# A mixture-of-experts encoder step: one 128-slot expert in the middle, experts in a table's order, 8 KB rows for the down weights

## What is computed

```
logits = h @ w_router + b_router                      # [384, 32]
top_val, top_idx = lax.top_k(logits, 4)               # 4 of 32 experts for each token
gates = softmax(top_val)
# for each expert e that a token chose:
gu = xblk @ w_gate_up[e] + b_gate_up[e]               # [1024] -> [2048]
x_glu, x_lin = jnp.split(gu, 2, axis=-1)              # clamped at 7
act = x_glu * sigmoid(1.702 * x_glu) * (x_lin + 1.0)
y += gates * (act @ w_down[e] + b_down[e])            # [1024] -> [1024]
```

## Time and profile before

| | us |
|---|---|
| median of 3 runs | 1396.67 |
| the profiled execution | 1392.92 |
| its span, first to last instruction | 1391.1 |
| PE busy | 1257.7 (90%) |
| DVE busy | 410.3 (29%) |
| ACT busy | 233.4 (17%) |
| weight loads, queue 1 | 77.6% of 16 DMA engines' span |

### The profile page before, as it was taken

How to read it: one execution, slowest core, us unless ns; L and a number is a source line. 1 busy time by engine, 2 the same in 40 slices (tenths; PEclk the granted TensorE clock), 3 DMA queues, 4 the chain that set the end, 5 groups by cost and what they waited for, 6 DMA issues and landing times.

```text
span 1391.1 us, 16030 instructions
## 1 busy us (share of the span) xinstructions
PE 1257.7 (90%) x5950; PEld 601.2 (43%) x5950; DVE 410.3 (29%) x849; ACT 233.4 (17%) x455; POOL 176.4 (13%) x153
## 2 busy tenths in 40 slices
PE   3997689899899999999999999999999999999696
PEld 2564468775734434334343324434333443425232
DVE  3496853411441321213212122221212222121223
ACT  0117634323211011010110101001010101100002
POOL 1099824325300000000000000000000000000000
PEclk8998699889799999999999999999999999999898
DMA  9222022003699999999999999999999999999991
GB/s 322 82 81 90 11 82 76 1 8 140 231 399 418 418 418 418 418 416 417 418 418 418 418 417 417 418 418 418 419 417 416 417 418 418 418 418 416 417 391 54
DMA packets 91374, 446.13 MB, mean 321 GB/s; under 512 B 9072, under 2 KB 14448, under 8 KB 57456
## 3 DMA queue, kind: packets, MB, share of 16 engines
q1 hardware_dynamic: 87168, 436.66, 77.6%
q10 hardware_dynamic: 3376, 5.99, 1.3%
q0 software_dynamic: 800, 3.08, 0.7%
HBM read 441.05 MB, written 4.65 MB: 320 GB/s over the span
## 4 chain that ended last, share of the span: by engine, by line
PE 45%; DMA 23%; SPq 18%; DVE 4%; issue 4%; POOL 3%; ACT 2%; ACTq 0%; DVEq 0%; POOLq 0%
DMA ring<-in_w_gate_up 22%; PE bank L1542 11%; SPq L413 10%; PE bank L1562 8%; SPq L417 8%; PE bank L1510 7%; PE bank L1228 5%; PE bank L1435 3%; DMA win<-in_w_in 2%; POOL ring L351 2%; PE bank L1524 2%; POOL cb L475 1%; DVE qkvc L858 1%; PE bank L1315 1%; PE bank L1336 1%
## 5 line engine op out<-in xcount | busy, mean ns | idle before, releaser
L1542 PE MATMUL bank<-ring,win 128*64 128x512 f32 x2112 | 480.6, 598 | 42.6 <-DMA ring<-in_w_gate_up 42.5
L1542 PEld LDWEIGHTS bank<-ring,win 128*64 128x64 f32 x2112 | 143.5, 137 | 361.2 <-issue 222.4
L1562 PE MATMUL bank<-ring,win 128*64 128x512 f32 x1056 | 239.5, 607 | 1.6 <-issue 0.8
L1116 DVE TENSOR_SCALAR win<-bank 128x512 f32<-128x512 f32 x33 | 22.8, 692 | 706.7 <-PE bank L1542 706.7
L1228 PE MATMUL bank<-hT,win 128*128 128x384 f32 x384 | 132.9, 508 | 20.7 <-DMA win<-in_w_in 9.6
L1562 PEld LDWEIGHTS bank<-ring,win 128*64 128x64 f32 x1056 | 74.7, 139 | 152.5 <-issue 149.7
L1228 PEld LDWEIGHTS bank<-hT,win 128*128 128x128 f32 x384 | 76.1, 200 | 75.2 <-issue 17.0
L770 ACT ACTIVATE win<-win 128x512 f32<-128x512 f32 x32 | 20.2, 630 | 500.8 <-DVE win L1116 500.8
L1510 PEld LDWEIGHTS bank<-win,qkvc 128*128 128x128 f32 x816 | 95.9, 196 | 14.3 <-issue 13.0
L1510 PE MATMUL bank<-win,qkvc 128*128 128x128 f32 (+1 forms) x816 | 100.4, 281 | 1.2 <-DVE win L1051 1.2
L1524 PE MATMUL bank<-win 128*128 128x512 f32 x192 | 89.2, 601 | 0.8 <-DVE win L1194 0.8
(11 more groups left out here) (269 smaller groups left out, 923.4 us busy)
## 6 DMA issues: line engine op xcount, KB each, us to landing
ring<-in_w_gate_up SPq DMA_DIRECT2D x264, 1024.0 KB, 20.5
ring<-in_w_down SPq DMA_DIRECT2D x132, 1024.0 KB, 22.9
win<-in_w_in SPq DMA_DIRECT2D x4, 2048.0 KB, 8.2
win<-in_w_in SPq DMA_DIRECT2D x4, 1024.0 KB, 17.9
win<-in_w_out SPq DMA_DIRECT2D x2, 2048.0 KB, 9.4
out_ss<-ring POOLq DMA_DIRECT2D x1, 2048.0 KB, 11.9
hT<-in_xT SPq DMA_DIRECT2D x1, 1536.0 KB, 10.7
out_y<-xt SPq DMA_DIRECT2D x3, 512.0 KB, 2.7
```

The source lines that it names most:

```text
L1542: mm = pe.matmul(bank[half][a * BLK:(a + 1) * BLK], xs[:, k], ring[:, c:c + 512], start=False, stop=(k == KD - 1), skip_group_check=True)
L1562: mm = pe.matmul(bank[7][a * BLK:(a + 1) * BLK], actT[:, (k % 4) * P + (k // 4) * BLK:][:, 0:BLK], ring[:, c:c + 512], start=(k == 0), sto ...
```

## The change

The pairs become 15 (`NPAIR`), in 17 units (`NU`): units 0 to 7 are pairs at positions 0 to 15, unit 8 (`MID`) is one expert with 128 slots at position 16 (`WIDE`), units 9 to 15 are pairs at positions 17 to 30, and unit 16 is one expert of 64 slots at position 31. DVE finds the fullest of experts 2 to 31 (`places_of_units`) and swaps it with expert 16; a table `expert_no` gives the expert of each position, and SP reads an entry of it before each turn's loads from position 2 on. The fullest expert no longer counts as over 64 in the table of extra blocks (over 128 it still would). The extra loops stand behind unit 14 as before, now counted with `s_tabs` 2. In the wide unit each k multiplies both halves of the slots before its ring slot is released, into banks 0, 1, 4 and 5; its `down` writes banks 7 and 3. A down slot's partition p gets rows 2p and 2p+1, one piece of 8 KB, and `turn_act` reads the columns of `a_s` two apart to match.

```
-NPAIR = NE // 2
+NPAIR = (NE - 2) // 2
+NU = NPAIR + 2
+MID = NPAIR // 2 + 1
+WIDE = 2 * MID
...
+        a_rows = a_s.rearrange("p (b r two) -> p b r two", b=2, two=2)
...
+        WIDE_COMBINE = (2, 3, 0, 1, 2, 3)
+        WIDE_BANK = 3
```

SP, the loads:

```
-                        src = w_down[bass.ds(e, 1), r0:r0 + 2 * P, :].rearrange("a (k p) n -> (a p) k n", p=P)
-                        ld.dma_start(dst.rearrange("p (k n) -> p k n", k=2), src).then_inc(s_w[s], 16)
+                        src = w_down[bass.ds(e, 1), r0:r0 + 2 * P, :].rearrange("a (p k) n -> (a p) (k n)", p=P)
+                        ld.dma_start(dst, src).then_inc(s_w[s], 16)
...
-            with sp.Fori(1, NE - 2) as e:
-                load_expert(sp, e, lambda s: e * USES + (USED[s] - USES))
-
+            load_expert(sp, 1, lambda s: USED[s])
             sp.wait_ge(s_tabs, 1)
+            with sp.Fori(2, NE - 3) as e:
+                number = sp.value_load(expert_no[0:1, bass.ds(e, 1)], min_val=0, max_val=NE - 1)
+                load_expert(sp, number, lambda s: e * USES + (USED[s] - USES))
+
...
+            for e in (NE - 3, NE - 2, NE - 1):
+                number = sp.value_load(expert_no[0:1, e:e + 1], min_val=0, max_val=NE - 1)
+                load_expert(sp, number, lambda s: n_extra * USES + ((e - 1) * USES + USED[s]))
```

DVE and (the first six lines) ACT:

```
+            def wide_unit():
+                sigmoid(2 * MID)
+                sigmoid(2 * MID + 1)
+                rows_high(MID + 1)
+                gates_t(MID)
+                rows_out(0, 7, WIDE)
+                rows_out(1, WIDE_BANK, WIDE)
...
+            def places_of_units():
+                link(dve.memset(big[:, 0:2], 0.0))
+                link(dve.scalar_tensor_tensor(key, cntB, 2.0 * NE, iota[:, 0:NE], ALU.mult, ALU.subtract))
+                link(dve.tensor_reduce(topkey, key[:, 2:NE], AX_X, ALU.max))
+                link(dve.tensor_scalar(big[:, 2:NE], key[:, 2:NE], topkey, None, ALU.is_equal))
+                link(dve.tensor_scalar(rest, big, -1.0, 1.0, ALU.mult, ALU.add))
...
+                link(dve.tensor_scalar(expert_at[:, WIDE:WIDE + 1], bigno, float(WIDE), None, ALU.add))
+                link(dve.tensor_copy(expert_no, expert_at))
+                dve.tensor_scalar(sel_at[0:3 * NE], expert_at[0:3 * NE], cst[0:3 * NE, X_ROW:X_ROW + 1], None,
+                                  ALU.is_equal).then_inc(s_tabs, 1)
...
+                link(dve.tensor_tensor(nxb, nxb, rest, ALU.mult))
...
+            def wide_unit():
+                dve.wait_ge(s_hp, MID + 1)
+                gate_hits_one(WIDE, P)
+                dve.wait_ge(s_hg, MID + 1)
+                dve.wait_ge(s_xg5, MID + 1)
+                row_hits(pos_at, WIDE + 1)
+                clamp(WIDE, s_g, s_lin)
+                swiglu(s_sig, item + 1, s_g, item + 1, s_lin, item * 2 + 2, s_act)
+                turned(s_att, item + 1, s_atr)
+                clamp(WIDE, s_g, s_lin, low=4)
+                for o in (0, 1):
+                    add(o, WIDE_COMBINE[o], s_cmb, MID * 6 + (o + 1), s_add)
+                swiglu(s_sig, item + 2, s_g, item + 2, s_lin, item * 2 + 4, s_act)
+                for o in range(2, 6):
+                    add(o, WIDE_COMBINE[o], s_cmb, MID * 6 + (o + 1), s_add)
+                turned(s_att, item + 2, s_atr, to=actT_wide)
...
+            places_of_units()
+            pair(0, 0, 0, lambda: row_hits(pos_at, 2), (2, 3), tables)
+            with dve.Fori(1, MID - 1) as u:
+                pair(u, 2 * u, 2 * u, lambda: row_hits(pos_at, 2 * u + 2), (2 * u + 2, 2 * u + 3))
+            pair(MID - 1, WIDE - 2, WIDE - 2, lambda: row_hits_one(WIDE, P), (WIDE, WIDE))
+            wide_unit()
+            with dve.Fori(MID + 1, NU - 2) as u:
+                pair(u, 2 * u - 1, 2 * u - 1, lambda: row_hits(pos_at, 2 * u + 1), (2 * u + 1, 2 * u + 2))
```

PE:

```
-                    mm = pe.transpose(bank[6][:, j * P:(j + 1) * P], a_s[:, j * P:(j + 1) * P], mat("ident"))
+                    mm = pe.transpose(bank[6][:, j * P:(j + 1) * P], a_rows[:, j // 2, :, j % 2], mat("ident"))
...
+            def wide_unit():
+                for x in range(2):
+                    bias_rows(sel_sb[:, x], bank[4 * x], 0)
+                    bias_rows(sel_sb[:, x], bank[4 * x + 1], F)
+                for k in range(KD):
+                    pe.wait_ge(s_w[SLOT_OF[k]], WIDE * 16 + 16)
+                    for x in range(2):
+                        for half in range(2):
+                            for a in range(2):
+                                c = SLOT_OF[k] * SLOT + half * F + a * 512
+                                mm = pe.matmul(bank[4 * x + half][a * BLK:(a + 1) * BLK], xTe[:, k, x * BLK:(x + 1) * BLK],
+                                               ring[:, c:c + 512], start=False, stop=(k == KD - 1), skip_group_check=True)
+                                if k == KD - 1 and x == 1:
+                                    mm.then_inc(s_wu, 1)
+                    if k < KD - 1:
+                        mm.then_inc(s_wu, 1)
+                pe.wait_ge(s_gtc, MID)
+                pe.wait_ge(s_yc, item * 2)
+                pe.wait_ge(s_add, MID * 6)
+                for o in (0, 1):
+                    combine(o, gT, y_s, s_cmb, WIDE_COMBINE)
+                turn_act(s_act, item + 1, s_att)
+                for o in (2, 3):
+                    combine(o, gT, y_s, s_cmb, WIDE_COMBINE)
+                pe.wait_ge(s_add, MID * 6 + 2)
+                for o in (4, 5):
+                    combine(o, gT, y_s, s_cmb, WIDE_COMBINE)
+                pe.wait_ge(s_hp, MID + 2)
+                pe.wait_ge(s_lin, item * 2 + 3)
+                rows(range(6), hp, P)
+                pe.wait_ge(s_atr, item + 1)
+                turn_act(s_act, item + 2, s_att)
+                rows(range(6, KD), hp, P).then_inc(s_xg5, 1)
+                pe.wait_ge(s_atr, item + 2)
+                pe.wait_ge(s_hg, MID + 1)
+                turn_gates()
+                pe.wait_ge(s_add, MID * 6 + 6)
+                for k in range(KD):
+                    if k % 2 == 0:
+                        pe.wait_ge(s_w[KD + k // 2], WIDE * 16 + 16)
+                    for x, (aT, b) in enumerate(((actT, 7), (actT_wide, WIDE_BANK))):
+                        for a in range(2):
+                            c = (KD + k // 2) * SLOT + (k % 2) * D + a * 512
+                            mm = pe.matmul(bank[b][a * BLK:(a + 1) * BLK], aT[:, (k % 4) * P + (k // 4) * BLK:][:, 0:BLK],
+                                           ring[:, c:c + 512], start=(k == 0), stop=(k == KD - 1), skip_group_check=True)
+                            if k == KD - 1 and x == 1:
+                                mm.then_inc(s_wu, 1)
+                    if k % 2 == 1 and k < KD - 1:
+                        mm.then_inc(s_wu, 1)
...
+            pair(0, True, 0)
+            with pe.Fori(1, MID) as u:
+                pair(u, False, 2 * u)
+            wide_unit()
+            with pe.Fori(MID + 1, NU - 2) as u:
+                pair(u, False, 2 * u - 1)
...
+            pair(NU - 2, False, n_extra + (NE - 3), ahead=BLK)
+            item, turn = 2 * NU - 2, n_extra + (NE - 1)
+            first_expert(NU - 1, False, turn)
+            pe.wait_ge(s_atr, item + 1)
+            pe.wait_ge(s_hg, NU)
+            turn_gates()
+            down(turn, s_atr, item + 1)
+            pe.wait_ge(s_gtc, NU)
+            pe.wait_ge(s_yc, item * 2 + 2)
+            pe.wait_ge(s_add, 6 * NU)
             for o in range(6):
-                combine(o, gT, y_s, s_cmb)
+                combine(o, gT[0:BLK], y_s[0:BLK], s_cmb)
```

More of the change, by code:

```diff
@@ L197, in stream_step @@
         xTe = wscratch(KD * P).rearrange("p (k s) -> p k s", k=KD)
-        g_s, l_s, sg_b, t_s, a_s, actT = (wscratch(512) for _ in range(6))
+        g_s, l_s, sg_b, t_s, a_s, actT, actT_wide = (wscratch(512) for _ in range(7))
+        a_rows = a_s.rearrange("p (b r two) -> p b r two", b=2, two=2)
         y_s = wscratch(D).rearrange("p (a n) -> p a n", a=2)
@@ L221, in stream_step @@
         if8 = srow(NT * 8).rearrange("p (n j) -> p n j", n=NT)
-        gate = srow(NT * NE).rearrange("p (n e) -> p n e", n=NT)
+        both = srow(2 * NT * NE).rearrange("p (q e) -> p q e", q=2 * NT)
+        pos, gate = both[:, 0:NT], both[:, NT:2 * NT]
+        placed = srow(2 * NT * NE).rearrange("p (q e) -> p q e", q=2 * NT)
+        pos_at, gate_at = placed[:, 0:NT], placed[:, NT:2 * NT]
+        big, rest, key = srow(NE), srow(NE), srow(NE)
+        topkey, bigno = srow(1), srow(1)
+        expert_at = srow(NE)
+        expert_no = srow(NE).bitcast(I32)
+        sel_at = srow(NE)
+        swap = cb[:, NX * NE:NX * NE + 2 * NT * NE].rearrange("p (q e) -> p q e", q=2 * NT)
         gsum = srow(NT)
@@ L1190, in _ @@
                                 add(o, COMBINE_BANK[o], x_pe, x_at(i, T_COMBINE, T_ACT + o + 1), x_dve)
-            pair(NPAIR - 1, True, n_extra + (NE - 2))
+            pair(NU - 2, NE - 3, n_extra + (NE - 3), lambda: row_hits_one(NE - 1, BLK), (NE - 1,))
```

(57 more changed lines are left out.)

176 lines of the change are left out of this document (97 added, 79 removed).

## The result

The changed kernel took **1354.29 us** (median of 4 runs, 1353.57 to 1355.27) against 1396.62 (4 runs, 1395.48 to 1397.97) beside it: ratio 0.9692, 95% interval 0.9675 to 0.9708. The forecast was 1347.6 us: right in sign, the time inside the range, 6.7 us too low. The profiled execution took 1354.15 us; its span is 1352.3, where the prediction had 1342.0.

What follows compares the result with a forecast made beforehand. The prediction held that weight loads set the pace, with PE late only at the end. Its terms, -30.1 - 15.4 - 10.6 + 7 = -49.1 us, took 1396.67 to 1347.6 us, range 1339 to 1361.

Steps and rivals of the forecast that it cites:

- One turn less and a PE that is no longer late: Expert loop and its end: 32 turns of loads instead of 33, -30.1 us, and last `down` sooner at full clock, -15.4.
- the 1.7 us that it put to the full clock: Last `down`: runs at full clock in 7.1 us, not 8.8, so -1.7 us within the -15.4.
- 8 KB rows: Down-weight loads: rate rises to gate/up's 422 GB/s, 0.35 us a turn over 30 turns, -10.6 us, bounds 0 and -13.
- The transposes that read columns two apart: PE's transposes of the activations: bounded by 0 and a doubling of 0.66 us for four, taken as 0.
- The wide unit: Unit with 128 slots: PE's longer work on one turn's loads lets the queue run dry, +7 us, bounds +2 and +16.
- the 44.8 us of the sum: Work left in the load queue, counted from the start of the wide unit's gate/up, before it runs dry.
- dry to 48.3, then 3.5 us for each slot: Wide unit: queue dry from 44.8 to 48.3 us, then three slots 3.5 apart instead of 2.5: 6.5, taken as +7.
- Loop steps not taken: Before the last pair: PE runs six untaken steps, some 5.2 us, covered by slack; taken as 0, bounds 0 to +4.
- 1: Rival on down loads: the 8 KB rows gain nothing, 1358 us; chance 0.15.
- 2: Rival on the wide unit: its chains wait some 23 us more, dry queue gives back the saved load, 1371 us; chance 0.07.
- 3: Rival on the pairs' loops: 13 loop ends each cost PE 6.9 us (1358 us) or twice that (1449); chance 0.03.
- 4: Rival on the swap: one block is left to the extra loops, still 33 turns, 1393 us; chance 0.02.

Runs made afterwards that it cites:

- the padded kernel: Changed kernel plus 48 more 128 x 128 matmuls on the matrix of ones at the start of PE's program: 1352.19 us, ratio 0.9689.
- three pairs of kernels: 4 KB against 8 KB down rows: kernel before (8 KB: 0.9942), changed kernel (4 KB: 0.9738), kernel before without extra block (0.9663 with 4 KB, 0.961 with 8 KB).
- the four kernels made from before: Kernel before itself (1396.62 us), with 8 KB rows (1386.18), without the extra block (1347.70), and with both (1340.52).
- the ten made from after: Changed kernel, its rerun, and eight variants (4 KB rows, 1 or 12 loop steps, longer or shorter gap, rows behind down, padded, shorter gap with 1 step): 1349.62 to 1359.38 us.
- the pair of rows8 kernels: 8 KB down rows alone in the kernel before: 1386.18 us, ratio 0.9942; and undone to 4 KB in the changed kernel: 1358.14 us, 0.9738.

## Why the prediction was right, and where its sum was off

The mechanism held: the loads bound the kernel, a turn fewer is worth a turn, and the late PE of the extra block goes with it. The sum missed the span by 10.3 us:

1. **One turn less and a PE that is no longer late**, -45.5: measured -45.0 by leaving the block out alone (-31.2 and -13.8). Right. But the 1.7 us that it put to the full clock are no gain by themselves: without the block and with the old order at the end `down` starts 6.4 us behind the start of the last k and runs 8.63 us, in the padded kernel 8.0 behind it and 7.09. What the combines ahead of `down` save in clock they cost in its start: from the last k to the end it is 29.3 us (1312.03 to 1341.3) and 29.4 (1321.04 to 1350.4).
2. **8 KB rows**, -10.6: measured -8.2 to -9.5 of loads in three pairs of kernels, and -6.8 to -7.1 from the first gate/up to the end. The mechanism was right, the size off by 1.1 to 2.4 us in the loads and 3.5 in all. I took 0.35 a turn from two short stretches; the paces of 60.24 us a pair before and 59.65 after give 0.3 a turn, 9 us. The long stretch was the better one. The transposes that read columns two apart, taken as 0, cost next to nothing: four take 0.64 us, before 0.60. And I counted the whole gain at the end, where two pairs of kernels have a late PE and the third a slower last `down`.
3. **The wide unit**, +7: measured 9.1 to 9.8. The 15 us between gate/up and `down` came as worked out. Both ends of the dry stretch were mis-sized. Its end: I let it stop with the four down slots, but the rate is still 383 GB/s from 910 to 920, because the next gate/up slots also come free late. Its start: PE's last wait for a slot ahead of the wide unit, and three stretches of 1 us around the gap in the loads:

```profile
833.06 1.94 PE L1650 MATMUL bank<-ring,win 128*64 128x512 f32 x8 [0.55 <-DMA ring<-in_w_gate_up]
```

```profile
891.00:892.00 1.00, 1.00 (x8) 0.48 (x8) 0.36 (x3) 0.91 (x2) 0.00 (x0) 1.00 0.28 115
...
895.00:896.00 1.00, 1.00 (x6) 0.29 (x4) 0.00 (x0) 0.00 (x0) 0.00 (x0) 1.00 0.00 0
896.00:897.00 1.00, 1.00 (x8) 0.34 (x6) 0.00 (x0) 0.00 (x0) 0.00 (x0) 1.00 0.76 147
```

No load moved between 892 and 896 us. 892 is some 43 us behind the start of the wide gate/up (848.74), about 1 us sooner than the 44.8 of the sum, while the loads came back some 48 us behind it, as worked out. So in 890 to 900 us 6.1 us are lost, where the sum's own terms (dry to 48.3, then 3.5 us for each slot) give 4.4. Some 0.8 of it can be read: the 15.0 to the last landing came from a turn with 4 KB rows, 0.3 us longer, and PE entered the wide unit 15.7 us behind its last wait (833.06), where a steady turn has 15.2. The price hangs on the whole way to the next gate/up.

4. **Loop steps not taken**, taken as 0, bounds 0 to +4: 1.0 to 2.4 us. This step failed in its reasoning. I spread the 6.9 us that PE stood before the last pair over eight steps and called the six left 5.2, as if a step had a price. It has no one price: six cost 1.6 or 7.3 us by where they lie. And the slack that was to cover them was not there in full: from the loop to the end PE waited for no load.
5. **Ahead of the experts**: not in the sum, +2.9 in the two profiled executions. The start falls between 378.7 and 384.2 in the four kernels made from before, 378.7 and 386.4 in the ten made from after: scatter alone can make the 2.9, but these few executions don't show that the change has no part in it.

Four kernels show the sum without the split's 1 us: from the first gate/up to the end 1007.6 us before, 962.6 without the block, 955.5 with 8 KB rows besides, 966.0 with the wide unit. That is -45.0, -7.1 and +10.5 against -45.5, -10.6 and +7: 0.5, 3.5 and 3.5 us, the last of them the wide unit and the loop together. With the 2.9 ahead they make up the 10.3, within rounding. That the forecast lay only 6.7 us off is part luck: at the median 3.6 us less are missing, since the profiled execution of before lay 3.7 us under its median and that of after 0.1.

The rivals: 1 falls by the pair of rows8 kernels; 2 by 9.4 us of dry loss, not 23; 3 (dear loop ends of the pairs) by the pace of 59.65, with no such gap inside the pairs' loops; its thought, that a loop can cost PE by more than its instructions, came true in the one place where I had priced it at nothing. 4 falls by 256 loads.

## What to carry to other kernels

Where a queue of loads sets the pace, price an added stall by what it does to the queue, up to the point where slots come free at the old pace again, and not up to the first slot. An idle time named "issue" at a loop is not a price per step: move the loop by some instructions before you count on it. And where single executions scatter by more than the effect, split the span at events in the trace (first expert, last load, end) and compare the parts.
